# Routing of thirteen tiles moved into the merge stage, and a first gather from expert 0's ranks alone

## Chip, cores and metric

The kernel runs on one core of a Trainium2 chip. The metric is the device time of one execution in microseconds (us).

## The reference, cut to what matters

One encoder layer: two token mixers (banded attention and stick-breaking attention) are merged by gates and projected, then a hierarchical mixture of experts is added. 2048 tokens of width 1024, 4 groups of 8 experts, hidden width 512. Blocks of 128 rows are formed expert by expert.

```python
x = x + (merged @ w_out[layer]).astype(x.dtype)
h2 = rms_norm(x, norm_ffn_g[layer])
...
g_top, g_idx = lax.top_k(g_prob, 1)                  # one group of four
e_top, e_idx = lax.top_k(jax.nn.softmax(e_logits), 2)  # two experts of its eight
e_top = e_top / jnp.sum(e_top, axis=-1, keepdims=True)
weights = (g_top * e_top).reshape(-1)
counts = jax.ops.segment_sum(jnp.ones_like(eid), eid, num_segments=N_EXPERTS)
padded = (counts + ROW_BLOCK - 1) // ROW_BLOCK * ROW_BLOCK
dest = pad_offsets[s_eid] + jnp.arange(n_assign) - offsets[s_eid]
...
return (jax.nn.silu(xr @ w1[e]) * (xr @ w3[e])) @ w2[e]   # per block of 128 rows
```

## The kernel before

The layer runs as four programs one behind the other, each a block with a stream of instructions for each engine: norm and values, projection with banded attention, stick-breaking with gates, the merge stage, and last routing with the experts. This change touches the last two. Every product of the heavy kind is three matmuls (`passes3`), of operands split into a rounded part and a rest (hi, lo) of type fp32r; ScalarE (ACT) rounds, VectorE (DVE) takes the rest.

**Merge stage** (`merge_and_output_projection`). 16 tiles of 128 tokens. For tile n VectorE adds the residual (L1454), ACT and VectorE form the norm, TensorE (PE) turns x (`turn`) and multiplies by the router's weights (`route`), and VectorE takes the 36 logits of each token (L1465). Between these lie the units of the branch products, which end with tile 12 (`units_after`): behind it VectorE and ACT have little to do while TensorE works on `quarter` after `quarter`. In tiles 12 to 14 the first six of eight up-weight pieces of expert 0 are loaded by SP, rounded by ACT (L1412) and split by VectorE (L1511), two to a tile (`early_after`). SP loads piece j only when piece j-2 has been split. `m_lo`, `y_hi` and `y_lo` are tiles of this stage.

**Routing** (`routing_and_experts`, VectorE's list from L1866). On all 16 tiles at once VectorE picks the group and two experts of each token (`first_max` and what is between, 20 chained steps: `Chain` puts a semaphore wait behind each), marks them in OH and their sum O (L1884, L1887, bf16), and TensorE makes from O the counts of each expert (L2018, 16 matmuls with a matrix of ones) and the rank of each token within its expert (L2020, L2022, 16 matmuls), bf16 operands. From these come the number of blocks of each expert, their offsets, and the destination of each row: `lo` is its place in a block, `hi` its block. `row1h` are one-hots of lo (L1926, four instructions of 1024 columns). 32 matmuls of two columns (L2029) sum the tokens of block 0; from them comes the index column of the first gather (L1935), which GpSimd (POOL) issues (L1747). Then for four groups of 8 of the 32 (choice, tile) pairs VectorE makes block one-hots (L1942, 512 columns) and their product with token and weights (L1946, 1536 columns), and TensorE sums them into the table of all blocks (`table(m)`, L2036). VectorE then reads the table (`table()`, L1951 to L1954).

**Experts** (`all_experts`). For each block: TensorE turns the gathered rows (L2046), ACT rounds them (L1806), VectorE splits them (L1959), then up products (L52 to L54 into `ex_ps_h`), silu (L1824), gate (L1979), down products. The weights of the next expert stream in through SP (12 pieces of 512 KB an expert). A piece is loaded when the piece that held its place has been split: L1726 loads expert 1's up pieces and waits for `up_split` for the last two, L1729 loads its down pieces and waits for `down_split`, all in SP's order. ACT rounds expert 1's down pieces (L1819) between its two silus of block 0. What sets the order everywhere is each engine's list as written; no planner changes it.

TensorE's order ahead of the experts: table(0) to table(2), turn of block 0, table(3). VectorE's: four groups of marks, first_up(6), split of x, table(), first_up(7), four down pieces.

## Time and profile before

| what | us |
|---|---|
| median of 3 runs | 2675.66 (2674.98 to 2676.53) |
| the profiled execution | 2677.67 |
| its span | 2675.8 |
| TensorE busy in the span | 2584.5 |
| VectorE busy in the span | 1639.0 |
| ScalarE busy in the span | 1490.5 |

All times of the trace count from the start of the span. Matmul durations overlap, so what counts for a row of them is the distance of their starts. The granted clock is that of TensorE, 1.00 for 2.4 GHz and 0.50 for 1.2 GHz. A "DMA share" of 1 is all 16 DMA engines busy.

### The profile page before, as it was taken

Reading aid. Unit: us, or ns where it says so; the run is one execution under the profiler, and the core shown is the slowest. Engines: PE = TensorE matmul, PEld = TensorE weight load, DVE = VectorE, ACT = ScalarE, POOL = GpSimd, SP = SyncE. Lnnn points to the kernel's source line nnn. Section 1 sums busy time; section 2 is a strip of 40 time slices with the busy share of each in tenths; the row PEclk is TensorE's granted clock in tenths of the full one; section 3 lists DMA queues with packets and bytes.
Section 4 is the critical chain, followed back from the end, with each engine's and each line's share of the span. In section 5 each row is a group of like instructions: output and inputs, shape, how many; then the busy total and the mean of one; then the engine's idle time right before and its main releaser. Section 6 shows DMA issues by size and latency. Waiting matters only on the chain. (4 is left out here: it accounts for less than half of the span.)

```text
span 2675.8 us, 41251 instructions
## 1 busy us (share of the span) xinstructions
PE 2584.5 (97%) x13573; PEld 2157.3 (81%) x13574; DVE 1639.0 (61%) x2218; ACT 1490.5 (56%) x2630; POOL 612.3 (23%) x707
## 2 busy tenths in 40 slices
PE   7999999989999999999899999699999999999997
PEld 6788777778888888888899998577788888888886
...
GB/s 179 132 206 149 126 122 134 145 278 220 196 216 169 188 174 195 194 141 112 228 157 120 134 126 123 170 289 389 323 228 234 243 287 317 324 235 224 228 302 65
DMA packets 197344, 536.67 MB, mean 201 GB/s; under 512 B 20136, under 2 KB 70776, under 8 KB 192736
## 3 DMA queue, kind: packets, MB, share of 16 engines
...
q14 instruction: 50, 0.41, 0.0%
...
## 5 line engine op out<-in xcount | busy, mean ns | idle before, releaser
L1078 POOL TENSOR_TENSOR sb_sig<-sb_sig,sb_R 128x512 f32<-128x512 f32 (+1 forms) x320 | 340.7, 1065 | 409.5 <-DVE sb_R L1018 409.3
L52 PE MATMUL ex_ps_h<-w_region,ex_x_hi 128*128 128x512 f32 x816 | 322.9, 396 | 0.8 <-DVE ex_x_lo L1959 0.8
L54 PE MATMUL ex_ps_h<-w_region,ex_x_lo 128*128 128x512 f32 x816 | 318.8, 391 | 0.0
L53 PE MATMUL ex_ps_h<-w_region,ex_x_hi 128*128 128x512 f32 x816 | 318.6, 390 | 0.0
L1964 DVE TENSOR_TENSOR w_region<-ex_w,w_region 128x1024 fp32r<-128x1024 f32 x248 | 284.9, 1216 | 1.8 <-ACT w_region L1812 1.7
L1018 DVE TENSOR_TENSOR_SCAN sb_R<-sb_z,sb_R,sb_zeros 128x512 f32<-128x512 f32 x192 | 245.7, 1279 | 57.1 <-ACT sb_z L946 56.9
L1969 DVE TENSOR_TENSOR ex_wd_lo<-ex_w,ex_wd_hi 128x1024 fp32r<-128x1024 f32 x200 | 239.6, 1219 | 38.8 <-ACT ex_wd_hi L1819 38.8
L1812 ACT CAST w_region<-ex_w 128x1024 fp32r<-128x1024 f32 x248 | 240.2, 1053 | 9.7 <-DMA ex_w<-in_w_exp 9.4
L958 ACT CAST sb_aT_hi<-sb_pst 128x512 fp32r<-128x512 f32 (+1 forms) x320 | 168.1, 525 | 134.2 <-PE sb_pst L1107 130.9
L1026 DVE TENSOR_TENSOR sb_aT_lo<-sb_pst,sb_aT_hi 128x512 fp32r<-128x512 f32 (+1 forms) x320 | 192.3, 601 | 51.9 <-ACT sb_aT_hi L958 50.0
L945 ACT ACTIVATE sb_sig<-sb_z 128x512 f32<-128x512 f32 (+1 forms) x320 | 172.2, 538 | 85.2 <-PE sb_z L1100 83.8
L1819 ACT CAST ex_wd_hi<-ex_w 128x1024 fp32r<-128x1024 f32 x196 | 196.8, 1060 | 2.2 <-DMA ex_w<-in_w_exp 2.2
L52 PE MATMUL ip_ps<-h_hi,ip_w_hi 128*128 128x512 f32 x448 | 182.4, 407 | 3.5 <-DVE ip_w_lo L605 3.5
L54 PEld LDWEIGHTS ex_ps_h<-w_region,ex_x_lo 128*128 128x128 f32 x816 | 153.6, 188 | 32.3
L52 PEld LDWEIGHTS ex_ps_h<-w_region,ex_x_hi 128*128 128x128 f32 x816 | 153.6, 188 | 31.5 <-issue 1.0
L53 PEld LDWEIGHTS ex_ps_h<-w_region,ex_x_hi 128*128 128x128 f32 x816 | 153.8, 188 | 30.6
L1107 PE MATMUL sb_pst<-sb_ident,sb_sig 128*128 128x128 f32 x1088 | 171.6, 273 | 7.0 <-DVE sb_aT_lo L1026 7.0
L54 PE MATMUL ip_ps<-h_hi,ip_w_lo 128*128 128x512 f32 x448 | 175.8, 392 | 0.0
L53 PE MATMUL ip_ps<-h_lo,ip_w_hi 128*128 128x512 f32 x448 | 175.4, 392 | 0.0
L1107 PEld LDWEIGHTS sb_pst<-sb_ident,sb_sig 128*128 128x128 f32 x1088 | 137.6, 140 | 46.1 <-issue 7.9
L946 ACT ACTIVATE sb_z<-sb_z 128x512 f32<-128x512 f32 (+1 forms) x320 | 171.7, 537 | 0.0
...
## 6 DMA issues: line engine op xcount, KB each, us to landing
...
```

The source lines that it names most:

```text
L52: nc.tensor.matmul(out, w_hi, x_hi, start=first, stop=False)
L53: nc.tensor.matmul(out, w_hi, x_lo, start=False, stop=False)
L54: return nc.tensor.matmul(out, w_lo, x_hi, start=False, stop=last)
L945: nc.scalar.activation(sig[:, j % 5, 0:width], z[:, j % 3, 0:width], ACT.Sigmoid, scale=HD ** -0.5)
L1018: nc.vector.tensor_tensor_scan(R[:, r, first + 1:first + width + 1], z[:, j % 3, 0:width], zeros[:, 0:width], start, ALU.mult, ALU.max).th ...
L1026: nc.vector.tensor_tensor(aT_lo[part], ps_t[:, j % 2, b0 * P:TC].rearrange("p (b s) -> p b s", s=P), aT_hi[part], ALU.subtract).then_inc(l ...
L1078: nc.gpsimd.tensor_tensor(sig[:, j % 5, 0:width], sig[:, j % 5, 0:width], R[:, r, first:first + width], ALU.mult).then_inc(a_done, 1)
L1107: last = nc.tensor.transpose(ps_t[:, j % 2, b * P:(b + 1) * P], sig[:, j % 5, b * P - OFF[j]:(b + 1) * P - OFF[j]], ident[:, :])
L1812: nc.scalar.copy(wu_hi[:, j, :], wr[:, j, :]).then_inc(up_rounded, 1)
L1819: nc.scalar.copy(wd_hi[:, u, k, :], wr[:, KD + k, :]).then_inc(down_rounded, 1)
L1964: nc.vector.tensor_tensor(wu_lo[:, j, :], wr[:, j, :], wu_hi[:, j, :], ALU.subtract).then_inc(up_split, 1)
L1969: nc.vector.tensor_tensor(wd_lo[:, u, k, :], wr[:, KD + k, :], wd_hi[:, u, k, :], ALU.subtract).then_inc(down_split, 1)
```

## The change

The choosing of experts for tiles 0 to 12 (`NTA` = 13) and the one-hots of their ranks move into the merge stage, into the gaps of VectorE behind tile 12; TensorE forms their ranks there (`rank`, ahead of the last tile's product), and forms them a second time at the start of the last program. The tiles OH, O, tri, ones, first and row1h now live in `w_low`, a region that both stages share, and are fp32r instead of bf16. The last program chooses for three tiles only. The first gather takes its rows from the ranks of expert 0 alone: block 0 holds the tokens whose rank in expert 0 is under 128, so no block count is needed, and it has an index tile of its own. Every expert gets at least one block as before. `row1h` of all tiles is one-hot of the rank's low seven bits. In the marking of blocks two instructions for a group become 24 `tensor_scalar` instructions, one for each (tile, component). The order ahead of the experts changes on TensorE (turn first, then all four tables) and on VectorE (two groups of marks, split of x, two groups, table(), down pieces, then both first_ups). The semaphore `y_half_done` goes, its counts move into `br0_done`.

The core of the diff:

```diff
+NTA = NT - 3
...
+            def split_early(j):
+                dve.wait_ge(up_rounded, j + 1)
+                nc.vector.tensor_tensor(w64[:, 1, j, :], up_slots[j % 2], w64[:, 0, j, :],
+                                        ALU.subtract).then_inc(up_split, 1)
+
+            chain = Chain(dve, chosen)
+            NA = 2 * NTA
+            d, lo = (spare[:, NTA * NE + i * NA:NTA * NE + (i + 1) * NA] for i in (0, 2))
+            di = spare[:, NTA * NE + NA:NTA * NE + 2 * NA].bitcast(I32)
+            kept = spare[:, NTA * NE + NA:NTA * NE + 2 * NA].rearrange("p (k t) -> p k t", k=2)
+
+            def rank_rows():
+                V = nc.vector
+                by_expert = spare[:, 0:NTA * NE].rearrange("p (t e) -> p t e", t=NTA)
+                dve.wait_ge(ranked, 1)
+                for k in range(2):
+                    chain(V.tensor_tensor(by_expert, ps_r, OH[:, k, 0:NTA, :, :].rearrange("p t g e -> p t (g e)"), ALU.mult))
+                    chain(V.tensor_reduce(d[:, k * NTA:(k + 1) * NTA], by_expert, AX.X, ALU.add))
+                chain(V.tensor_copy(di, d))
+                chain(V.tensor_single_scalar(di, di, P - 1, ALU.bitwise_and))
+                chain(V.tensor_copy(lo, di))
+                chain(V.scalar_tensor_tensor(kept, d.rearrange("p (k t) -> p k t", k=2), float(P),
+                                             OH[:, :, 0:NTA, 0, 0], ALU.is_lt, ALU.mult))
+                chain(V.tensor_tensor(first, kept.unsqueeze(3).to_broadcast([P, 2, NTA, 2]),
+                                      cst[:, C_TOK:C_TOK + NTA].unsqueeze(1).unsqueeze(3).to_broadcast([P, 2, NTA, 2]),
+                                      ALU.mult))
+
+            def mark_rows():
+                shape = [P, NTA, P]
+                for k in range(2):
+                    chain(nc.vector.tensor_tensor(row1h[:, k, 0:NTA, :],
+                                                  cst[:, C_IOTA:C_IOTA + P].unsqueeze(1).to_broadcast(shape),
+                                                  lo[:, k * NTA:(k + 1) * NTA].unsqueeze(2).to_broadcast(shape),
+                                                  ALU.is_equal))
...
+                if n == NTA:
+                    nc.vector.tensor_copy(tri, cst[:, C_TRI:C_TRI + P])
+                    chain(nc.vector.tensor_copy(ones, cst[:, C_ONES:C_ONES + P]))
+                    mark_experts(nc, chain, OH, O, ohg, oh, 0, NTA).then_inc(O_ready, 1)
+                    split_early(1)
+                if n == NTA + 1:
+                    rank_rows()
+                    split_early(4)
+                if n == NTA + 2:
+                    split_early(5)
...
-                for j in early_after(n):
-                    dve.wait_ge(up_rounded, j + 1)
-                    nc.vector.tensor_tensor(w64[:, 1, j, :], up_slots[j % 2], w64[:, 0, j, :],
-                                            ALU.subtract).then_inc(up_split, 1)
+                if n == NTA - 1:
+                    dve.wait_ge(l_read, NTA)
+                    ohg, oh = choose_experts(nc, chain, logits, cst, 0, NTA, spare, y_flat)
+                    split_early(0)
+                if n == NTA:
+                    split_early(2)
+                    split_early(3)
+                if n == NTA + 1:
+                    mark_rows()
...
+            def rank():
+                pe.wait_ge(weighted, NU)
+                pe.wait_ge(O_ready, 1)
+                nc.tensor.matmul(ps_r, tri, O[:, 0:NTA, :], start=True, stop=False)
+                for t in range(NTA - 1):
+                    last = nc.tensor.matmul(ps_r[:, t + 1:, :], ones,
+                                            O[:, t, :].unsqueeze(1).to_broadcast([P, NTA - 1 - t, NE]),
+                                            start=False, stop=t == NTA - 2)
+                last.then_inc(ranked, 1)
...
+                if n + 2 == NT:
+                    rank()
...
+def routing_views(low):
+    kept = low[:, 0, :, :].rearrange("p k c -> p (k c)")
+    n_oh, n_o = 2 * NT * NE, NT * NE
+    at = n_oh + n_o
+    OH = kept[:, 0:n_oh].rearrange("p (k t g e) -> p k t g e", k=2, t=NT, g=GR)
+    O = kept[:, n_oh:at].rearrange("p (t e) -> p t e", t=NT)
...
+    row1h = low[:, 1, :, :].rearrange("p k c -> p (k c)").rearrange("p (k t r) -> p k t r", k=2, t=NT)
+    return OH, O, tri, ones, first, first_late, late1h, row1h
...
+def choose_experts(nc, ch, logits, cst, t0, t1, real, hot):
+    V, n = nc.vector, t1 - t0
+    bc = lambda ap, width: ap.to_broadcast([P, n, width])
+    cut = lambda ap, at, w: ap[:, at:at + n * w].rearrange("p (t e) -> p t e", t=n)
+    es, key8, key4 = cut(real, 0, EG), cut(real, n * EG, EG), cut(real, n * EG, GR)
...
+    ohg, oh = cut(hot, 0, GR), [cut(hot, n * GR, EG), cut(hot, n * (GR + EG), EG)]
+    G = logits[:, t0:t1, 0:GR]
+    E = logits[:, t0:t1, GR:GR + NE].rearrange("p t (g e) -> p t g e", g=GR)
+    rev4, rev8 = cst[:, C_REV4:C_REV4 + GR], cst[:, C_REV8:C_REV8 + EG]
+
+    def first_max(out1h, src, m, key, rev, width):
+        ch(V.tensor_reduce(m, src, AX.X, ALU.max))
+        ch(V.tensor_tensor(key, src, bc(m.unsqueeze(2), width), ALU.is_equal))
+        ch(V.tensor_tensor(key, key, bc(rev.unsqueeze(1), width), ALU.mult))
+        ch(V.tensor_reduce(gk, key, AX.X, ALU.max))
+        ch(V.tensor_tensor(out1h, key, bc(gk.unsqueeze(2), width), ALU.is_equal))
+
+    first_max(ohg, G, gm, key4, rev4, GR)
+    ch(V.tensor_tensor(G, G, bc(gm.unsqueeze(2), GR), ALU.subtract))
+    ch(V.tensor_tensor(E, E, ohg.unsqueeze(3).to_broadcast([P, n, GR, EG]), ALU.mult))
+    ch(V.tensor_reduce(es, E.rearrange("p t g e -> p t e g"), AX.X, ALU.add))
+    first_max(oh[0], es, mx0, key8, rev8, EG)
+    ch(V.scalar_tensor_tensor(es, oh[0], -3.0e38, es, ALU.mult, ALU.add))
+    first_max(oh[1], es, mx1, key8, rev8, EG)
+    ch(V.tensor_tensor(logits[:, t0:t1, NE], mx1, mx0, ALU.subtract))
+    return ohg, oh
...
+def mark_experts(nc, ch, OH, O, ohg, oh, t0, t1):
+    V, shape = nc.vector, [P, t1 - t0, GR, EG]
+    for k in range(2):
+        ch(V.tensor_tensor(OH[:, k, t0:t1, :, :], ohg.unsqueeze(3).to_broadcast(shape),
+                           oh[k].unsqueeze(2).to_broadcast(shape), ALU.mult))
+    flat = [OH[:, k, t0:t1, :, :].rearrange("p t g e -> p t (g e)") for k in range(2)]
+    return V.tensor_tensor(O[:, t0:t1, :], flat[0], flat[1], ALU.add)
...
-            pool.wait_ge(table_step, FIRST_COLUMN)
-            fetch(0)
+            pool.wait_ge(ix_x_ready, 1)
+            nc.gpsimd.sem_inc(pool_order, 1)
+            nc.gpsimd.indirect_dma_start(xg[:, :], None, h2_d, bass.IndirectOffsetOnAxis(ap=ix_x[:, 0:1], axis=0)) \
+                .then_inc(x_in, 16)
...
+            ohg, oh = choose_experts(nc, ch, logits, cst, NTA, NT, wide, sel)
+            mark_experts(nc, ch, OH, O, ohg, oh, NTA, NT).then_inc(O_ready, 1)
+            dve.wait_ge(O_ready, 1)
+            V.tensor_tensor(first_late, bc(O[:, late, 0:1], [P, NT - NTA, 2]), bc(tok[:, late].unsqueeze(2), [P, NT - NTA, 2]),
+                            ALU.mult)
+            for cols in (slice(0, 1), slice(MAXB + 1, BT)):
+                V.tensor_scalar(idx_all[:, cols], iota[:, cols], 0.0, trash, ALU.mult, ALU.add)
+            V.memset(w_all[:, 0:1], 0.0)
+
+            dve.wait_ge(summed, RANKED)
+            V.tensor_tensor(late1h, bc(iota.unsqueeze(1), [P, NT - NTA, P]), bc(ps_r[:, late, 0:1], [P, NT - NTA, P]),
+                            ALU.is_equal).then_inc(hot_ready, 1)
+            ch(V.tensor_scalar(nblk, ps_c[:, 0:NE], 1.0, float(P - 1), ALU.max, ALU.add))
             ch(V.tensor_copy(di, nblk))
             ch(V.tensor_single_scalar(di, di, 7, ALU.logical_shift_right))
             ch(V.tensor_copy(nblk, di))
             ch(V.tensor_tensor_scan(ends, cst[:, C_ONES:C_ONES + NE], nblk, 0.0, ALU.mult, ALU.add))
             ch(V.tensor_tensor(off, ends, nblk, ALU.subtract))
+
+            dve.wait_ge(summed, FIRST_SUMMED)
+            ch(V.tensor_scalar(tmp[:, 0:1], ps_f[:, 0:1], 0.0, trash1, ALU.is_equal, ALU.mult))
+            V.scalar_tensor_tensor(ix_x[:, :], ps_f[:, 0:1], -1.0, tmp[:, 0:1], ALU.add, ALU.add).then_inc(ix_x_ready, 1)
             V.tensor_copy(blk_tab[:, NE:2 * NE], ends[0:1, :])
+            V.tensor_copy(blk_tab[:, 0:NE], off[0:1, :]).then_inc(table_step, 1)
+            dve.wait_ge(exp_out, 2)
+            ch(V.tensor_reduce(gtop, gs, AX.X, ALU.add))
+            ch(V.tensor_scalar(sd, ed, 1.0, None, ALU.add))
+            ch(V.scalar_tensor_tensor(dest, bc(off.unsqueeze(1), [P, NT, NE]), float(P), ps_r, ALU.mult, ALU.add))
             for k in range(2):
+                ch(V.tensor_tensor(by_expert, dest, OH[:, k, :, :, :].rearrange("p t g e -> p t (g e)"), ALU.mult))
                 ch(V.tensor_reduce(d[:, k * NT:(k + 1) * NT], by_expert, AX.X, ALU.add))
             ch(V.tensor_copy(di, d))
             V.tensor_single_scalar(hi_i, di, 7, ALU.logical_shift_right)
             ch(V.tensor_single_scalar(lo_i, di, P - 1, ALU.bitwise_and))
             V.tensor_copy(hi, hi_i)
             ch(V.tensor_copy(lo, lo_i))
+            shape = [P, 2, NT - NTA, P]
+            V.tensor_tensor(row1h[:, :, late, :], bc(iota.unsqueeze(1).unsqueeze(1), shape),
+                            bc(lo.rearrange("p (k t) -> p k t", k=2)[:, :, late].unsqueeze(3), shape),
+                            ALU.is_equal).then_inc(hot_ready, 1)
+            V.reciprocal(gtop, gtop)
+            ch(V.reciprocal(sd, sd))
+            ch(V.tensor_tensor(w[:, 0, :], gtop, sd, ALU.mult))
+            for k in range(2):
+                V.tensor_copy(vals[:, k, :, 0], tok)
+            ch(V.tensor_tensor(w[:, 1, :], w[:, 0, :], ed, ALU.mult))
             ch(V.tensor_copy(vals[:, :, :, 1], w[:, :, :]))
             ch(V.tensor_tensor(vals[:, :, :, 2], w[:, :, :], vals[:, :, :, 1], ALU.subtract))
+
+            def mark_blocks(m):
+                k, part = GROUPS[m]
                 if m >= 2:
                     dve.wait_ge(hot_used, m - 1)
+                for i in range(GA):
+                    t = part * GA + i
+                    for c3 in range(3):
+                        last = V.tensor_scalar(rows1h[:, m % 2, i, c3, :], iota[:, 0:64], hi[:, k * NT + t:k * NT + t + 1],
+                                               vals[:, k, t, c3:c3 + 1].bitcast(F32), ALU.is_equal, ALU.mult)
+                last.then_inc(hot_ready, 1)
 
             def table():
+                dve.wait_ge(h2_stored, NT * 16 + 32)
                 dve.wait_ge(hot_used, NA // GA)
...
-            first_up(NEARLY)
+            mark_blocks(0)
+            mark_blocks(1)
             split_x(0)
+            mark_blocks(2)
+            mark_blocks(3)
             table()
-            for j in range(NEARLY + 1, KD):
-                first_up(j)
             for k in range(KF):
                 down_piece(0, 0, k)
+            for j in range(NEARLY, KD):
+                first_up(j)
             dve.wait_ge(table_step, BOUNDS)
...
+            late, NL = slice(NTA, NT), NT - NTA
+            nc.tensor.matmul(ps_r[:, 0:NTA, :], tri, O[:, 0:NTA, :], start=True, stop=False)
+            for t in range(NTA - 1):
+                nc.tensor.matmul(ps_r[:, t + 1:NTA, :], ones, O[:, t, :].unsqueeze(1).to_broadcast([P, NTA - 1 - t, NE]),
+                                 start=False, stop=t == NTA - 2)
+            for t in range(NTA):
+                nc.tensor.matmul(ps_r[:, late, :], ones, O[:, t, :].unsqueeze(1).to_broadcast([P, NL, NE]),
+                                 start=t == 0, stop=False)
+            for t in range(NTA):
+                nc.tensor.matmul(ps_c[:, 0:NE], ones, O[:, t, :], start=t == 0, stop=False)
+            for k in range(2):
+                for t in range(NTA):
+                    nc.tensor.matmul(ps_f, row1h[:, k, t, :], first[:, k, t, :], start=k == t == 0, stop=False)
             pe.wait_ge(O_ready, 1)
+            nc.tensor.matmul(ps_r[:, late, :], tri, O[:, late, :], start=False, stop=False)
+            for t in range(NTA, NT - 1):
+                nc.tensor.matmul(ps_r[:, t + 1:, :], ones, O[:, t, :].unsqueeze(1).to_broadcast([P, NT - 1 - t, NE]),
+                                 start=False, stop=t == NT - 2)
+            for t in range(NTA, NT):
+                last = nc.tensor.matmul(ps_c[:, 0:NE], ones, O[:, t, :], start=False, stop=t == NT - 1)
             last.then_inc(summed, 1)
+            pe.wait_ge(hot_ready, 1)
+            for i in range(NL):
+                last = nc.tensor.matmul(ps_f, late1h[:, i, :], first_late[:, i, :], start=False, stop=i == NL - 1)
             last.then_inc(summed, 1)
 
             def table(m):
+                k, part = GROUPS[m]
+                pe.wait_ge(hot_ready, m + 3)
                 for i in range(GA):
+                    last = nc.tensor.matmul(ps_b[:, 0:192], row1h[:, k, part * GA + i, :],
                                             rows1h[:, m % 2, i, :, :].rearrange("p c b -> p (c b)"),
+                                            start=m == i == 0, stop=m == len(GROUPS) - 1 and i == GA - 1)
                 last.then_inc(hot_used, 1)
 
...
-            for m in range(NA // GA - 1):
+            turn_x(0)
+            for m in range(len(GROUPS)):
                 table(m)
-            turn_x(0)
-            table(NA // GA - 1)
             pe.wait_ge(table_step, BOUNDS)
             all_experts(pe, lambda e, first: None, rows)
```

## Rows read from the trace of the kernel before

**Rows 1.** Table of stretches: us, busy us of each engine (instructions), granted clock, DMA share.

```profile
1716.00:1721.00 5.00, 4.21 (x32) 2.54 (x32) 3.63 (x20) 5.00 (x6) 0.00 (x0) 0.54 1.03 401
1721.00:1726.00 5.00, 0.00 (x0) 0.00 (x0) 4.72 (x12) 0.50 (x1) 0.00 (x0) 0.80 0.77 304
1726.00:1734.00 8.00, 6.99 (x32) 6.90 (x32) 4.78 (x12) 0.00 (x0) 0.00 (x0) 0.50 0.00 1
1734.00:1747.00 13.00, 9.40 (x40) 8.70 (x40) 11.55 (x11) 1.01 (x1) 2.24 (x2) 0.50 0.19 54
1747.00:1751.00 4.00, 3.30 (x8) 2.63 (x9) 3.93 (x8) 0.00 (x0) 1.72 (x2) 0.50 0.42 110
1807.00:1927.00 120.00, 115.50 (x535) 92.60 (x534) 96.09 (x101) 87.57 (x108) 26.84 (x31) 1.00 0.98 368
1927.00:2647.00 720.00, 720.00 (x3419) 599.37 (x3418) 503.75 (x548) 463.51 (x587) 151.73 (x205) 1.00 0.75 252
```

**Rows 2.** VectorE in order of time, new block: start, us, line, operands; idle before in brackets.

```profile
1703.09 0.26 DVE L1465 SCALAR_TENSOR_TENSOR logits<-mo_ps_l,mo_small,rt_bias 128x36 f32<-128x36 f32 x1 [1.45 <-PE mo_ps_l L1575]
1707.18 0.22 DVE L1866 TENSOR_REDUCE w_stage<-logits 128x16 f32<-128x64 f32 x1 [3.84 <-PEq L1188]
...
1713.99 0.17 DVE L1881 TENSOR_TENSOR w_stage<-w_stage 128x16 f32<-128x16 f32 x1
...
1733.89 0.16 DVE L1935 SCALAR_TENSOR_TENSOR idx_all<-ex_ps_g,rt_cst 128x1 int32<-128x1 f32 x1
1733.97 0.68 DVE L1942 TENSOR_TENSOR w_stage<-rt_cst,ex_g 128x512 f32<-128x512 f32 x1
...
1743.91 1.22 DVE L1974 TENSOR_TENSOR w_region<-ex_w,w_region 128x1024 fp32r<-128x1024 f32 x1
1746.34 1.22 DVE L1959 TENSOR_TENSOR ex_x_lo<-ex_ps_x,ex_x_hi 128x1024 fp32r<-128x1024 f32 x1 [1.21 <-ACT ex_x_hi L1806]
```

**Rows 3.** TensorE: one line of its source view, then its timeline ahead of the experts.

```profile
L2029 PE MATMUL ex_ps_g<-rt_first,ex_wd_hi x32: 352/352/374, 1726.5 to 1733.2; 128*128 128x2 f32 x32
...
1741.53 2.02 PE L2036 MATMUL ex_ps_g<-ex_wd_lo,ex_wd_hi 128*128 128x192 f32 x8 [0.49 <-DVE ex_wd_lo L1946]
1743.35 1.91 PE L2046 MATMUL ex_ps_x<-ex_ident,w_stage 128*128 128x128 f32 x8
...
1747.70 0.79 PE L52 MATMUL ex_ps_h<-w_region,ex_x_hi 128*128 128x512 f32 x1 [0.79 <-DVE ex_x_lo L1959]
```

**Rows 4.** VectorE timeline: instructions with per-partition operand, then two without, neither pair chained.

```profile
399.00 0.88 DVE L565 SCALAR_TENSOR_TENSOR ba_qn<-ba_q,ba_gq,ba_rq 128x256 f32<-128x256 f32 x2 [4.70 <-ACT ba_rk L475]
399.80 0.41 DVE L567 SCALAR_TENSOR_TENSOR ba_kn<-ba_k,ba_gk,ba_rk 128x192 f32<-128x192 f32 x1
...
1724.52 0.18 DVE L1917 TENSOR_SCALAR ex_g<-ex_g 128x32 int32<-128x32 int32 x1
1724.61 0.17 DVE L1918 TENSOR_SCALAR ex_g<-ex_g 128x32 int32<-128x32 int32 x1
```

**Rows 5.** Last tiles of the merge stage: VectorE, then TensorE.

```profile
1657.54 0.43 DVE L1448 TENSOR_TENSOR mo_m_lo<-mo_gates,mo_m_hi 128x256 fp32r<-128x256 f32 x1
...
1666.82 1.23 DVE L1454 TENSOR_TENSOR mo_rows<-mo_ps,mo_rows 128x1024 f32<-128x1024 f32 x1 [2.81 <-PE mo_ps L54]
...
1683.37 0.50 PE L52 MATMUL mo_ps<-mo_wo_hi,mo_m_hi 128*128 128x512 f32 x1 [1.32 <-DVE mo_rows L1454]
```

**Rows 6.** Restart: VectorE, SP and ACT timelines, then a line of the DMA view.

```profile
1749.45 4.62 DVE L1969 TENSOR_TENSOR ex_wd_lo<-ex_w,ex_wd_hi 128x1024 fp32r<-128x1024 f32 x4
...
1707.53 2.77 SPq L1711 DMA_DIRECT2D ex_w<-in_w_exp  x6
...
1750.70 3.73 SPq L1729 DMA_DIRECT2D ex_w<-in_w_exp  x4
...
1762.07 1.05 ACT L1819 CAST ex_wd_hi<-ex_w 128x1024 fp32r<-128x1024 f32 x1 [1.22 <-DMA ex_w<-in_w_exp]
...
w_stage<-h,ex_ix_x POOLq DMA_INDIRECT x1, 5.2
```

161 lines of the change are left out of this document (42 added, 119 removed).

## The prediction

> **What bounds the kernel now.** I read the profile from the outside in. First the table of stretches: after 1927 us TensorE is busy in every one of 720 us, and from 1807 to 1927 it is busy for 115.5 of 120 us with the DMA engines at 0.98 [rows 1]. So what a change ahead of the experts saves or costs goes to the end of the kernel nearly whole, as an earlier or later start. The place of the change is the hole between the two: the last logits at 1703.09, the first instruction of the next block at 1707.18 [rows 2], the first expert matmul at 1747.70 [rows 3]. In this hole VectorE is the bound most of the time, as its list shows: twenty chained steps of choosing from 1707.18 to 1714.2, then ranks and one-hots, the index of the first gather at 1733.89, four groups of block marking from 1733.97 to 1743.91, the split of x at 1746.34 [rows 2]. TensorE waits for it, and runs at the lower clock, 1.2 GHz: granted 0.50 from 1726 to 1747 [rows 1].
>
> **What moves into the merge stage, and what it costs there.** Choosing for thirteen tiles is the same twenty steps on 13/16 of the columns: the fixed part stays, so 6.5 us for 7.0 [rows 2]. It starts when the last m is split (1657.97) and ends at about 1664.4; the split of the first expert piece behind it ends at 1665.7, and the next norm wants VectorE at 1666.82 [rows 5]. It is hidden by 1.2 us. The marking of experts (2.3 us), rank_rows (3.6) and mark_rows (two instructions of 1664 columns, 3.9 us) fall into the two like gaps of the next tiles; the pieces are loaded some microseconds later through SP's queue, since each load waits for a split, but they are wanted only by splits that the order has put later too. I take 0. If one of these covers were gone, the cost would be its overhang, 1 to 2 us. TensorE's rank() is thirteen matmuls with fp32 weights at the higher clock, 1.65 us, in a hole of 1.32 us ahead of the last tile [rows 5], which began at about 1682.05: **+0.3 us**.
>
> **The new block: TensorE first.** Choosing for three tiles takes VectorE 20 short steps of about 0.2 us and the marking 0.8 us, so O is ready at about 1712.4. But the index of the first gather waits for the ranks of all tiles (the semaphore summed), and they stand in TensorE's queue behind a prefix: 13 matmuls for the early ranks again, 13 for the late tiles' offset, 13 for the counts, 26 for the first rows. These are 65, and the operands are now fp32r, no longer bf16. The nearest rows: 32 matmuls with fp32r weights and 2 columns began from 1726.5 to 1733.2, one in (1733.2-1726.5)/31 = 0.216 us, at clock 0.50 [rows 1, 3]; with 192 columns eight took 2.02 us, hardly more. I price 61 at 0.216 and the four widest (416, 384, 352, 320 columns at 1.2 GHz) by their columns, 0.35 to 0.27, together 14.4 us: 1707.2 to 1721.6. Six more for the last tiles, 1.3 us, and a tail of 0.15: **ranks at 1723.1**, about 2 us later than before, where the 32 matmuls for them lie between 1716 and 1721 [rows 1], and VectorE idle for 10 us ahead of it. Behind this wait in VectorE's queue stands all the rest.
>
> **VectorE after that wait.** late1h (384 columns, 0.5 us), six chained steps to the block offsets (1.35), two for the index (0.45): the index is ready at 1725.4, 8.7 us earlier than the 1734.05 of before [rows 2]. Before the marking come five instructions of 512 columns at 0.72 with their gap (3.6 us; 0.69 is the 512-column row [rows 2]), one of 768 columns (0.9) and some fourteen short ones (2.8): 7.3 us, to 1732.7. What is the early gather worth? Its landing takes 5.2 us from issue [rows 6]; with 1.1 us on GpSimd it is in at 1731.7, turned at 1733.6 [rows 3], rounded at 1734.6. VectorE comes to split_x(0) only after two groups of marks, at about 1741. So the early gather is hidden anyway and I credit **nothing** for it.
>
> **The marks decide.** Before, a group is two instructions, and four groups took 1743.91-1733.97 = 9.94 us [rows 2]. After, a group is 24 tensor_scalar instructions of 64 columns, each with two per-partition operands, 96 in all. No row shows this form. Bounds: without such operands two tensor_scalars of 32 columns began 0.09 apart, at 1724.52 and 1724.61; with one, the instructions of 256 columns began 0.40 apart, which is 0.267 for the columns and 0.133 fixed [rows 4]. So one operand costs some 0.05. The low bound is 0.11 (none counts), with one counting 0.133+0.033 = 0.166, with two counting 0.22, and 0.25 if the 64 columns go at one in a cycle. I take 0.18, just above the row of one operand: 96 x 0.18 = **17.3 us, 7.3 more than before**.
> The Trainium skill, "Vector Engine (DVE) Microarchitecture Reference", section 5.2, gives about 75 ns fixed for an instruction and 1.04 ns a column; as an estimate 96 x 0.142 = 13.6 us, and my sum would end 3.7 us lower. The page "VectorE: DVE Perf Modes", in its rules for kernel authors, speaks against this part of the change: it says to keep the number of instructions small. The 0.09 us floor in the rows agrees with that.
>
> **The sum to the first expert matmul.** 1732.7 + 17.3 + 1.1 (split_x) = 1751.1; the last table(3) on TensorE, which now stands behind the last marks instead of beside the split, 2.0 [rows 3]; first expert matmul at 1753.2, against 1747.7: +5.5.
>
> **The restart of the weight stream.** Call T the start of VectorE's table(). Before T is 1747.5, and first_up(6) has run before it. After it, table (0.8), four down pieces at 1.13 (the row of four, 4.62 us), then both first_ups. SP's queue is in order: it waits for those two splits before it issues expert 1's last two up pieces and only then the four down pieces. So the two go at T+6.6 and T+7.7, the down pieces from T+8.2 about 0.45 apart (six issues in 2.77 us), the last at T+9.5. Before, the last was issued near 1754.1, T+6.6, and ACT could round it at 1762.07, 8.0 us later [rows 6]. The same 8.0 gives T+17.5 for T+14.6: ACT's rounding of it stands ahead of the second silu, so block 0 and the next loads of SP start 2.9 us later. With the DMA engines at 0.98 afterwards I don't let this be absorbed: **+3** (0 if the burst lands faster than the spread loads did, 5 if it collides with the first scatter).
>
> **Total**: 0.3 + 5.5 + 3.0 = +8.8 us. The profiled execution took 2677.67 with a span of 2675.8, 2.0 over the median of 2675.66. Difference on the median: **2684.5 us**.
>
> **Rivals.** (1) The clock. It rose once in this hole: during or right after the 32 rank and count matmuls between 1716 and 1721: 0.54 over these 5 us, 0.80 over the next 5. In the 32 with 2 columns, and in the 40 from 1734 to 1747, it stayed at 0.50 [rows 1, 3]. The prefix begins like the first and goes on like the second. If it rose 4.2 us in and stayed, the rest of the prefix halves: ranks at 1717.3, -5.8, **2678.6**, no change. The Trainium skill, "TensorE: Matmul & The Clock Gate", Part 1, says that sustained work releases the throttle; by it this rival is the likely one. The two runs at 0.50 speak against. (2) Cheap marks: 0.11 instead of 0.18, -6.7, **2677.7**, no change. The two 32-column instructions at 0.09 speak for it, the one-operand rows against. (3) Dear marks, 0.22 to 0.25: +3.8 to +6.7, about **2690**. (4) The other side, faster: TensorE at the higher clock from the prefix through to the experts. Then ranks come at 1714.6 (-8.5), table(3) takes half (-1.0), and the first matmuls of block 0, run at 0.50 until 1751, lose nothing (-1.7): -11.2, and it turns faster by 0.2% from marks at 0.15 down; with 0.133 it is -15.7, **2668.7**. Speaks against: before, the first matmuls of this block found the clock down, 0.54 over their stretch [rows 1]. (5) The chain moves and nothing comes of it: the DMA-bound stretch takes up a delay of the start, as its 4.5 us of idle TensorE suggest, **2676 to 2680**.
>
> **How the numbers follow.** A measurement of this kernel can tell about 0.2%, 5.4 us, from no change. My forecast (2681 to 2688.5) 0.44; (1) 0.13; (2) 0.12; (3) 0.14; (4) 0.10; (5) 0.07. Faster takes (4) and some luck elsewhere, 0.14; slower takes the forecast, (3) and no more, 0.58; same the rest, 0.28. The range for 8 in 10 leaves out the far ends of (3) and (4): 2671 to 2691.
>
> **What would show it.** Right: the first matmuls after the block start about 0.216 apart at granted clock 0.50, and the last of the counts near 1723; VectorE idle about 10 us ahead of late1h; the gather's index near 1725.4 but the first expert matmul later than 1747.7; 96 TENSOR_SCALAR records that take 16 to 21 us; expert 1's down pieces landing 17 us after table(). Wrong: PEclk at 1.00 between 1711 and 1723, marks under 13 us, a norm of tiles 13 to 15 that starts later than before (1666.82 and two more), or TensorE idle less in the first block than before.

## The result

The changed kernel takes 2692.18 us (median of 4, 2691.39 to 2693.13) against 2675.32 us before (4 runs, 2674.22 to 2676.53): ratio 1.0065, 95% interval 1.0052 to 1.0077. It is slower, by about twice what was forecast (+8.8 us), and its time lies 1.2 us beyond the range. The profiled execution has a span of 2691.3 us, 15.5 more than before.

VectorE of the changed kernel in order of time, from the start of the last program to table():

```profile
1706.30 0.17 DVE L1717 TENSOR_REDUCE ex_s<-logits 128x3 f32<-128x12 f32 x1 [2.39 <-PEq L1191]
...
1722.33 0.56 DVE L1991 TENSOR_TENSOR w_low<-rt_cst,ex_ps_h 128x384 fp32r<-128x384 f32 x1 [10.30 <-PE ex_ps_h L2130]
...
1724.41 0.16 DVE L2002 SCALAR_TENSOR_TENSOR ex_ix_x<-ex_ps_g,rt_cst 128x1 int32<-128x1 f32 x1
...
1731.86 10.79 DVE L2037 TENSOR_SCALAR ex_wd_hi<-rt_cst,ex_g,rt_vals 128x64 fp32r<-128x64 f32 x48
...
1743.70 10.79 DVE L2037 TENSOR_SCALAR ex_wd_hi<-rt_cst,ex_g,rt_vals 128x64 fp32r<-128x64 f32 x48
1756.68 0.28 DVE L2044 TENSOR_SCALAR rt_cst<-ex_ps_g,rt_cst 128x64 f32<-128x64 f32 x1 [2.18 <-PE ex_ps_g L2141]
```

They answer to [rows 2]. The choosing starts at 1706.30 and is done early, but VectorE then stands idle for 10.30 us until TensorE has the ranks (1722.33). The index of the first gather is there at 1724.57, 9.5 us earlier than before. The marks, 9.94 us before, are two rows of 48 instructions, 10.79 us each. Then TensorE, from its first matmul of the program, and the first expert matmul:

```profile
1706.60 0.69 PE L2112 MATMUL ex_ps_h<-w_low 128*128 128x416 f32 x1 [2.98 <-PEq L1191]
1707.08 2.84 PE L2114 MATMUL ex_ps_h<-w_low 128*128 128x384 f32 x12
1709.76 2.99 PE L2117 MATMUL ex_ps_h<-w_low 128*128 128x96 f32 x13
1712.55 2.92 PE L2120 MATMUL ex_ps_h<-w_low 128*128 128x32 f32 x13
1715.31 5.69 PE L2123 MATMUL ex_ps_g<-w_low 128*128 128x2 f32 x26
...
1756.73 0.79 PE L52 MATMUL ex_ps_h<-w_region,ex_x_hi 128*128 128x512 f32 x1 [0.17 <-issue]
```

These are the 65 prefix matmuls: the first 13 with 416 down to 32 columns, then 13, 13 and 26 that begin 0.21 us apart whether they have 96, 32 or 2 columns. The first expert matmul is at 1756.73 instead of 1747.70 [rows 3]. The restart of the weight stream, as VectorE, SP, GpSimd, ACT and TensorE show it (SP's row is expert 1's four down pieces, GpSimd's the first scatter, ACT's two round the second and the last of those down pieces, TensorE's is the first down product of block 0):

```profile
1762.08 2.35 DVE L2067 TENSOR_TENSOR w_region<-ex_w,w_region 128x1024 fp32r<-128x1024 f32 x2
...
1783.52 1.23 DVE L2052 TENSOR_TENSOR ex_x_lo<-ex_ps_x,ex_x_hi 128x1024 fp32r<-128x1024 f32 x1 [1.93 <-ACT ex_x_hi L1923]
...
1764.82 2.13 SPq L1846 DMA_DIRECT2D ex_w<-in_w_exp  x4
...
1765.55 1.62 POOL L1875 DMA_INDIRECT out_x<-w_stage,ex_ix_y  x1 [3.36 <-ACT w_stage L1964]
...
1774.61 1.04 ACT L1936 CAST ex_wd_hi<-ex_w 128x1024 fp32r<-128x1024 f32 x1 [2.10 <-DMA ex_w<-in_w_exp]
...
1777.88 1.05 ACT L1936 CAST ex_wd_hi<-ex_w 128x1024 fp32r<-128x1024 f32 x1 [0.21 <-DMA ex_w<-in_w_exp]
...
1777.38 0.79 PE L52 MATMUL ex_ps_y<-ex_wd_hi,ex_g_hi 128*128 128x512 f32 x1 [8.43 <-DVE ex_g_lo L2077]
```

VectorE's two late up splits end at 1764.43; SP, which waits for them, issues the last two up pieces and then the four down pieces at 1764.82, 0.7 us ahead of the scatter. Before, the last down piece was rounded at 1762.07 [rows 6], now at 1777.88. TensorE is idle for 8.43 us ahead of its first down product. That product needs the gated values g, and in ACT's list the rounding of their first half stands behind the second down piece of expert 1, which was rounded at 1774.61. The table of stretches (us, busy us of PE, PEld, DVE, ACT and POOL with instructions, granted clock, DMA share, GB/s):

```profile
1706.00:1722.00 16.00, 15.40 (x71) 15.42 (x71) 4.95 (x27) 10.14 (x11) 0.00 (x0) 0.50 0.91 347
1764.00:1778.00 14.00, 5.57 (x25) 4.26 (x24) 3.84 (x6) 4.20 (x6) 1.62 (x1) 0.79 0.83 262
1776.00:1780.00 4.00, 2.62 (x6) 2.01 (x7) 3.24 (x5) 2.37 (x3) 0.00 (x0) 0.50 0.20 76
1807.00:1927.00 120.00, 116.60 (x544) 94.35 (x542) 106.63 (x112) 96.80 (x117) 28.92 (x32) 1.00 1.03 387
```

The clock stays at 0.50 in the prefix, and behind the hole TensorE starts at 0.50 again. Because executions differ by some microseconds in when the last program starts, the runs are compared by distances from its first VectorE instruction. The last distance, to the end of the span, is of one execution each:

| run | ranks there (late1h) | first expert matmul | split of block 1's x | end of the span | time against the kernel before |
|---|---|---|---|---|---|
| before | | 40.5 | 59.1 | 968.6 | 1 |
| changed | 16.0 | 50.4 | 77.2 | 985.0 | 1.0065 (1.0052 to 1.0077) |
| a_marks2 | 16.0 | 38.9 | 66.2 | 973.9 | 1.0028 (1.0018 to 1.0038) |
| a_order | 16.0 | 50.5 | 70.8 | 979.3 | 1.0034 (1.0021 to 1.0046) |
| a_sporder | 16.1 | 50.5 | 67.1 | 978.2 | 1.0035 (1.0022 to 1.0047) |
| a_both | 16.0 | 38.9 | 56.5 | 966.4 | 0.9995 (0.9985 to 1.0005) |
| a_rankfirst | 10.5 | 44.9 | 71.4 | 979.2 | 1.0050 (1.0033 to 1.0066) |
| a_bf16 | 8.0 | 42.4 | 67.6 | 977.3 | 1.0043 (1.0029 to 1.0057) |
| a_lategather | 16.0 | 50.5 | 77.3 | 984.6 | 1.0066 (1.0049 to 1.0083) |
| b_marks24 | | 50.0 | 67.8 | 977.1 | 1.0041 (1.0027 to 1.0055) |
| best | 5.7 | 27.7 | 47.6 | 956.0 | 0.9962 (0.9949 to 0.9976) |

One thousandth is 2.7 us. All runs named a_ start from the changed kernel, b_ from the one before.

### The profile page after: what moved, and what is told of

The parts are those of the page before. It is cut to its first block and busy times, and to the rows that moved or that the text cites. A ratio compares the mean times of both kernels' runs of the same rounds, so it can differ in the third digit from the quotient of the medians.

```text
span 2691.3 us, 41412 instructions
## 1 busy us (share of the span) xinstructions
PE 2592.8 (96%) x13596; PEld 2167.7 (81%) x13597; DVE 1656.9 (62%) x2338; ACT 1490.9 (55%) x2628; POOL 611.4 (23%) x706
## 5 line engine op out<-in xcount | busy, mean ns | idle before, releaser
L2062 DVE TENSOR_TENSOR w_low<-ex_w,ex_wd_hi 128x1024 fp32r<-128x1024 f32 x200 | 239.6, 1219 | 46.1 <-ACT ex_wd_hi L1936 46.1
L52 PE MATMUL ex_ps_y<-ex_wd_hi,ex_g_hi 128*128 128x512 f32 x408 | 164.6, 403 | 9.2 <-DVE ex_g_lo L2077 9.2
```

The lines of the kernel that those rows point to most:

```text
L52: nc.tensor.matmul(out, w_hi, x_hi, start=first, stop=False)
L2062: nc.vector.tensor_tensor(wd_lo[:, u, k, :], wr[:, KD + k, :], wd_hi[:, u, k, :], ALU.subtract).then_inc(down_split, 1)
```

## Experiments: the marks

**a_marks2**, the changed kernel with two instructions for a group.

```diff
...
+                ch(V.tensor_tensor(blk1h, bc(iota[:, 0:64].unsqueeze(1), [P, GA, 64]),
+                                   bc(hi[:, own].unsqueeze(2), [P, GA, 64]), ALU.is_equal))
                 if m >= 2:
                     dve.wait_ge(hot_used, m - 1)
-                for i in range(GA):
-                    t = part * GA + i
-                    for c3 in range(3):
-                        last = V.tensor_scalar(rows1h[:, m % 2, i, c3, :], iota[:, 0:64], hi[:, k * NT + t:k * NT + t + 1],
-                                               vals[:, k, t, c3:c3 + 1].bitcast(F32), ALU.is_equal, ALU.mult)
-                last.then_inc(hot_ready, 1)
+                V.tensor_tensor(rows1h[:, m % 2, :, :, :], bc(blk1h.unsqueeze(2), [P, GA, 3, 64]),
+                                bc(val[:, own, :].unsqueeze(3), [P, GA, 3, 64]), ALU.mult).then_inc(hot_ready, 1)
```

> The changed kernel with the block marks made as before: two instructions a group (512 and 1536 columns) in place of 24 tensor_scalars. Theory M (the 24 instructions at 0.225 us each are the largest term): four groups take 10 us instead of 21.6, the first expert matmul comes 11.6 us earlier, at about 1745, and since the stream of weights restarts from VectorE's table() the end moves with it: about 2680.5 against 2692 of the changed kernel. Rival R (TensorE's tables and the order of the restart set the time whatever VectorE does): under 3 us gained.

```profile
1732.08 0.69 DVE L2038 TENSOR_TENSOR ex_wd_hi<-rt_cst,ex_g 128x512 fp32r<-128x512 f32 x1
1732.80 1.76 DVE L2042 TENSOR_TENSOR ex_wd_hi<-ex_wd_hi,rt_vals 128x1536 fp32r<-128x1536 f32 x1
...
1745.36 0.79 PE L52 MATMUL ex_ps_h<-w_region,ex_x_hi 128*128 128x512 f32 x1 [0.16 <-issue]
```

A group is 0.69 and 1.76 us again, and the first expert matmul comes 38.9 us after the start instead of 50.4: 11.5 us earlier, as expected. Of this the end shows 0.0037 of the time, 9.9 us (the difference of two ratios, each good to 3 us); in the two traces the last program is 11.1 us shorter. Rival R, under 3 us, falls.

**b_marks24**, the other way round: the kernel before with the 24 instructions alone.

```diff
-                ch(V.tensor_tensor(blk1h, bc(iota[:, 0:64].unsqueeze(1), [P, GA, 64]),
-                                   bc(hi[:, part].unsqueeze(2), [P, GA, 64]), ALU.is_equal))
...
+                for i in range(GA):
+                    a = m * GA + i
+                    for c3 in range(3):
+                        last = V.tensor_scalar(rows1h[:, v, i, c3, :], iota[:, 0:64], hi[:, a:a + 1],
+                                               val[:, a, c3:c3 + 1].bitcast(F32), ALU.is_equal, ALU.mult)
+                last.then_inc(hot_ready, 1)
```

> The kernel before with one part of the change alone: 24 tensor_scalars a group for the marks. Theory M: 21.6 us for four groups instead of 9.94, all of it on the path: 11.6 us slower, about 1.0043 of before. If part of the marks' cost in the changed kernel came from its other order: 8 us or less.

```profile
1730.04 21.48 DVE L1945 TENSOR_SCALAR ex_wd_lo<-rt_cst,ex_g,rt_vals 128x64 fp32r<-128x64 f32 x96
...
1753.92 0.79 PE L52 MATMUL ex_ps_h<-w_region,ex_x_hi 128*128 128x512 f32 x1 [1.21 <-DVE ex_x_lo L1959]
```

96 instructions in 21.48 us, 11.5 more than before, and the first expert matmul at 50.0 us instead of 40.5, so 9.5 of them are on the path: the marks begin 0.7 us sooner after the start, and the split of x, which had waited 1.21 us for ACT [rows 2], finds its operand ready. The whole is 11.0 us slower by the ratio (7 to 15 by its interval), 8.5 by the distance to the end of the span. The traces put it between the two expectations, and the ratio can't tell these apart. The marks alone so cost about as much as my whole forecast of +8.8.

**a_pointers** prices the instruction by its operands.

```diff
+                        a = hi[:, k * NT + t:k * NT + t + 1] if m in (0, 1) else -1.0
+                        b = vals[:, k, t, c3:c3 + 1].bitcast(F32) if m in (0, 2) else 0.0
+                        last = V.tensor_scalar(rows1h[:, m % 2, i, c3, :], iota[:, 0:64], a, b, ALU.is_equal, ALU.mult)
```

> Prices the disputed instruction by its operands. The changed kernel, with the 24 tensor_scalars of the four groups in four forms: group 0 with two per-partition operands as in the change, group 1 with the first one only (the factor is an immediate 0), group 2 with the second one only (the compared value is an immediate -1), group 3 with none. Groups 1 to 3 so mark nothing: the rows of three quarters of the (choice, tile) pairs are left out of the table. If each per-partition operand costs 0.058 us: 0.225, 0.166, 0.166 and 0.11 us an instruction, the four groups 5.4, 4.0, 4.0 and 2.6 us. If the first operand carries the whole price, groups 0 to 2 are alike. If the price lies in the 64 columns at one a cycle and not in the operands, all four are alike at 0.2 or more.

Its VectorE list, four rows of 24 with the split of x between:

```profile
1730.95 5.44 DVE L2039 TENSOR_SCALAR ex_wd_hi<-rt_cst,ex_g,rt_vals 128x64 fp32r<-128x64 f32 x24
1736.31 3.99 DVE L2039 TENSOR_SCALAR ex_wd_hi<-rt_cst,ex_g 128x64 fp32r<-128x64 f32 x24
...
1741.35 3.98 DVE L2039 TENSOR_SCALAR ex_wd_hi<-rt_cst,rt_vals 128x64 fp32r<-128x64 f32 x24
1745.24 2.53 DVE L2039 TENSOR_SCALAR ex_wd_hi<-rt_cst 128x64 fp32r<-128x64 f32 x24
```

Groups 1 to 3 of this kernel mark nothing, so three quarters of the rows are missing from its table, and only the length of these rows is read from it. From start to start a group of two operands takes 5.36 us, 0.223 an instruction; with either one alone 3.90 and 3.89, 0.163; with none (2.53-0.2)/23 = 0.10. So each per-partition operand costs 0.06 us, and the second as much as the first. This is the upper of the two bounds that I had (0.22), at the higher rate for the columns. The Trainium skill, "VectorE: DVE Perf Modes", tier table, gives tensor_scalar on fp32 in SBUF twice the rate of tensor_tensor. The trace agrees: without such operands 64 columns begin 0.10 us apart and the 32 columns of [rows 4] 0.09, so 32 columns more cost 0.01 to 0.02 us, where the tensor_tensor rows of 512 and 1536 columns (0.69 and 1.76 us) give 0.033. The Trainium skill, "Vector Engine (DVE) Microarchitecture Reference", section 5.2, gives about 75 ns fixed and 1.04 ns a column. As an estimate from both pages, 64 columns at twice that rate make 0.108 us, and the trace agrees for the form without such operands (0.10). By this estimate 96 marks would have been 10.4 us and not 21.6.

## Experiments: the restart of the weight stream

**a_order** puts VectorE's list behind the marks back.

```diff
             mark_blocks(3)
+            first_up(NEARLY)
             table()
+            for j in range(NEARLY + 1, KD):
+                first_up(j)
             for k in range(KF):
                 down_piece(0, 0, k)
-            for j in range(NEARLY, KD):
-                first_up(j)
```

> The changed kernel with VectorE's order behind the marks as before: first_up(6) ahead of table(), then table(), first_up(7), then the four down pieces. Nothing else moves. Theory B (the burst of six loads late in SP's queue costs what the trace shows: expert 1's last down piece rounded 21.2 us after table() instead of 14.6): 6 to 7 us gained, about 2685.5. Rival (my blind term of 3 us was right and the rest is the marks): 3 us, 2689. Second rival (DMA-bound stretch takes it up): 0 to 1 us.

SP's issues of expert 1's last two up pieces and four down pieces, and ACT's rounding of the last:

```profile
1756.01 3.45 SPq L1843 DMA_DIRECT2D ex_w<-in_w_exp  x2
1760.26 4.21 SPq L1846 DMA_DIRECT2D ex_w<-in_w_exp  x4
...
1772.21 1.05 ACT L1936 CAST ex_wd_hi<-ex_w 128x1024 fp32r<-128x1024 f32 x1 [0.39 <-DMA ex_w<-in_w_exp]
```

The pieces go out spread over 8.5 us, the last is rounded 15.2 us after table() instead of 21.2, and block 1's x is split 6.4 us earlier. The time is 8.3 us less by the ratios, and the distance to the end of the span 5.7 us less. So the part of the restart that this order makes is some 6 us, twice the 3 that I had for all of it.

**a_sporder** keeps VectorE's list and changes SP's only.

```diff
-            for j in range(KD):
-                if j >= NEARLY:
-                    sp.wait_ge(up_split, j + 1)
+            for j in range(NEARLY):
                 sp.dma_start(wr[:, j, :], w_pieces[NPC + j, :, :]).then_inc(w_in[j], 16)
             for k in range(KF):
...
+            for j in range(NEARLY, KD):
+                sp.wait_ge(up_split, j + 1)
+                sp.dma_start(wr[:, j, :], w_pieces[NPC + j, :, :]).then_inc(w_in[j], 16)
```

> The changed kernel, VectorE's order kept, but SP issues expert 1's four down pieces ahead of its last two up pieces. It tells whether the order of VectorE's splits or the blocking in SP's queue makes the burst. Theory B: the down pieces go out as each split ends, 1.1 us apart from about 2 us after table(), block 0 loses its hole of 7 us on TensorE: 5 to 7 us gained. Rival (the splits themselves are what block 0 waits for, through VectorE): under 2 us.

```profile
1758.16 3.73 SPq L1844 DMA_DIRECT2D ex_w<-in_w_exp  x4
1762.70 1.46 SPq L1847 DMA_DIRECT2D ex_w<-in_w_exp  x2
...
1767.37 2.17 ACT L1937 CAST ex_wd_hi<-ex_w 128x1024 fp32r<-128x1024 f32 x2 [0.25 <-DMA ex_w<-in_w_exp]
```

The four down pieces leave from 1758.16 on as each is split, the last is rounded by 1769.54, and block 1's x is split 10.1 us earlier than in the changed kernel. It is therefore the wait in SP's queue, ahead of four issues that had nothing to do with it, and not VectorE's own time. The time gains 8.0 us by the ratios, no more than a_order did, and the distance to the end of the span 6.8 of the 10.1 us: from 1807 to 1927, TensorE idles 5.0 us here and 3.4 us in the changed kernel. So some of what the start gains seems to be lost in the DMA-bound stretch; one execution each shows it.

**a_both** puts marks and VectorE's order back together (the two edits above).

> Marks as before and VectorE's order as before, the rest of the change kept. If the two terms add up: 11.6 + 6.5 = 18 us gained, about 2674, within 2 us of the kernel before: the early gather and the routing in the merge stage then bring nothing by themselves, since TensorE's fp32r prefix holds the ranks until 1722. If a third cost is hidden in the change: 2678 or more. If the part that was moved brings something: 2670 or less.

Ratio 0.9995 (0.9985 to 1.0005): no difference from the kernel before can be measured. The two terms add (9.9 + 8.3 = 18.2 of 18.7 us), and what else is in the change neither costs nor earns a net amount that can be measured. The first expert matmul comes 1.6 us earlier than before: that is what the moved routing, its prefix on TensorE, the early gather and TensorE's new order earn together.

## Experiments: why the moved routing earns so little

**a_rankfirst** puts the 26 two-column matmuls behind the ranks, and the index of the gather behind VectorE's chain.

```diff
-            for k in range(2):
-                for t in range(NTA):
-                    nc.tensor.matmul(ps_f, row1h[:, k, t, :], first[:, k, t, :], start=k == t == 0, stop=False)
             pe.wait_ge(O_ready, 1)
...
             last.then_inc(summed, 1)
+            for k in range(2):
+                for t in range(NTA):
+                    nc.tensor.matmul(ps_f, row1h[:, k, t, :], first[:, k, t, :], start=k == t == 0, stop=False)
             pe.wait_ge(hot_ready, 1)
```

> The changed kernel with TensorE's 26 two-column matmuls for block 0 moved behind the ranks and counts in its queue, and the gather's index computed by VectorE behind its routing chain, just ahead of the marks. Theory P (VectorE's 10.3 us of idle time are the fp32r prefix on TensorE, 0.216 us a matmul at the lower clock): the ranks come 5.6 us earlier, late1h at about 1716.7 instead of 1722.3, marks and first expert matmul 5.5 us earlier, about 2686.5 against 2692. Rival (VectorE waits for the late tiles' O or something else by then): late1h moves under 1 us.

```profile
1710.67 0.17 DVE L1717 TENSOR_REDUCE ex_s<-logits 128x3 f32<-128x12 f32 x1 [2.83 <-PEq L1191]
...
1721.15 0.55 DVE L1991 TENSOR_TENSOR w_low<-rt_cst,ex_ps_h 128x384 fp32r<-128x384 f32 x1 [4.75 <-PE ex_ps_h L2127]
```

This program started late, so only distances count: ranks 10.5 us after the start instead of 16.0, first expert matmul 44.9 instead of 50.4. Both moved by the 5.5 us expected, and the distance to the end of the span by 5.8. The time gained 4.0 us by the ratios, which within the intervals can't be told from 5.5.

**a_bf16** gives the rank and count matmuls bf16 operands.

```diff
+        O = sb("rt_O", [P, NT, NE], BF16)
+        tri_b, ones_b = sb("rt_tri", [P, P], BF16), sb("rt_ones", [P, P], BF16)
...
+            nc.scalar.copy(tri, cst[:, C_TRI:C_TRI + P])
+            nc.scalar.copy(ones, cst[:, C_ONES:C_ONES + P])
+            nc.scalar.copy(O[:, 0:NTA, :], O_early[:, 0:NTA, :].bitcast(F32)).then_inc(exp_out, 1)
...
+            pe.wait_ge(exp_out, 1)
```

> The changed kernel with bf16 copies of O, tri and ones for the rank and count matmuls of the last program (ACT makes them at its start, about 1 us; the 26 for block 0 stay fp32r and in place). Theory P: 39 of the 65 prefix matmuls go by their columns instead of 0.216 us, ranks 5 to 6 us earlier, about 2686.5. If the time of a small matmul does not depend on the type of its weights: plus 1 us from the copies, 2693.

TensorE's list, one stretch of the table, and VectorE's first instruction and late1h:

```profile
1710.57 2.29 PE L2121 MATMUL ex_ps_h<-rt_O,rt_ones 128*128 128x384 bf16 x12
1712.69 1.00 PE L2124 MATMUL ex_ps_h<-rt_O,rt_ones 128*128 128x96 bf16 x13
1713.53 0.48 PE L2127 MATMUL ex_ps_h<-rt_O,rt_ones 128*128 128x32 bf16 x13
1713.86 3.06 PE L2130 MATMUL ex_ps_g<-w_low 128*128 128x2 f32 x26
...
1714.00:1717.00 3.00, 3.00 (x32) 3.00 (x32) 0.94 (x6) 2.99 (x3) 0.00 (x0) 0.96 0.99 385
...
1709.28 0.17 DVE L1717 TENSOR_REDUCE ex_s<-logits 128x3 f32<-128x12 f32 x1 [2.19 <-PEq L1191]
...
1717.24 0.56 DVE L1997 TENSOR_TENSOR w_low<-rt_cst,ex_ps_h 128x384 fp32r<-128x384 f32 x1 [2.23 <-PE ex_ps_h L2137]
```

13 matmuls with 32 columns take 0.48 us in place of 2.92. And more than expected: the 26 with two columns, still fp32r, take 3.06 us in place of 5.69, since the granted clock was 0.96 (the 2.4 GHz level) over their stretch: it had risen by 1714, behind 38 bf16 matmuls in 3.3 us. The ranks and the first expert matmul come 8.0 us earlier, not 5.5, and the time is 5.9 us less by the ratios. With the fp32r prefix it had stayed at 0.50 for 16 us. So the clock rival was right in its mechanism and wrong for this kernel: the prefix as it was written did not bring the clock up, the bf16 one did. The Trainium skill, "TensorE: Matmul & The Clock Gate", Part 1, has sustained matmul activity release the throttle; by that rule alone the fp32r prefix would have been at 1.2 GHz only in its first part, and the table of the changed kernel speaks against it (0.50 from 1706 to 1722, with PE busy for 15.40 of 16 us). What it is in the two prefixes that makes the difference was not tried apart.

**a_lategather** undoes the early gather alone (VectorE computes the index behind its chain).

```diff
-            dve.wait_ge(summed, FIRST_SUMMED)
-            ch(V.tensor_scalar(tmp[:, 0:1], ps_f[:, 0:1], 0.0, trash1, ALU.is_equal, ALU.mult))
-            V.scalar_tensor_tensor(ix_x[:, :], ps_f[:, 0:1], -1.0, tmp[:, 0:1], ALU.add, ALU.add).then_inc(ix_x_ready, 1)
...
             ch(V.tensor_tensor(vals[:, :, :, 2], w[:, :, :], vals[:, :, :, 1], ALU.subtract))
+            dve.wait_ge(summed, FIRST_SUMMED)
+            ch(V.tensor_scalar(tmp[:, 0:1], ps_f[:, 0:1], 0.0, trash1, ALU.is_equal, ALU.mult))
+            V.scalar_tensor_tensor(ix_x[:, :], ps_f[:, 0:1], -1.0, tmp[:, 0:1], ALU.add, ALU.add).then_inc(ix_x_ready, 1)
```

> The changed kernel with the index of the first gather computed 7 us later, behind VectorE's routing chain and ahead of the marks. Theory (the early gather is hidden behind two groups of marks): within 1 us of the changed kernel, the index at about 1731.5 instead of 1724.5 and the first expert matmul where it was. If the early gather is worth what the change is named for: 5 to 7 us slower.

```profile
1731.82 0.16 DVE L2028 SCALAR_TENSOR_TENSOR ex_ix_x<-ex_ps_g,rt_cst 128x1 int32<-128x1 f32 x1
...
1737.36 1.94 PE L2151 MATMUL ex_ps_x<-ex_ident,w_stage 128*128 128x128 f32 x8 [13.60 <-DMA w_stage<-h,ex_ix_x]
```

The index is 7.4 us later, block 0 is turned 7.5 us later, and the first expert matmul is at 50.5 us after the start as before the edit; ratio 1.0066 against 1.0065. The early gather, the second thing that the change is named for, is worth nothing here.

**best** joins what was found: the edits of a_marks2, a_order, a_rankfirst and a_bf16, all marks and first_up(6) ahead of the split of x, and TensorE's turn of block 0 between table(1) and table(2).

```diff
-            mark_blocks(0)
-            mark_blocks(1)
-            split_x(0)
-            mark_blocks(2)
-            mark_blocks(3)
+            for m in range(len(GROUPS)):
+                mark_blocks(m)
+            first_up(NEARLY)
+            split_x(0)
...
-            turn_x(0)
             for m in range(len(GROUPS)):
+                if m == 2:
+                    turn_x(0)
                 table(m)
```

> All terms found put right at once: choosing and ranks in the merge stage as in the change; bf16 operands for ranks and counts; the 26 matmuls for block 0 behind them; index of the first gather behind VectorE's chain; marks by two instructions a group, all four ahead of the split of x; first_up(6) ahead of it too; order of the restart as before. If the terms add: ranks at 6 to 8 us after the block's start instead of 16, first expert matmul some 28 us after it (before: 40.5), and about 12 us less than the kernel before: 2663, ratio 0.9955. If the gather, now late, becomes what block 0 waits for: 3 us less gained. If the DMA-bound stretch behind takes it up: ratio 0.998 or more.

```profile
1705.34 0.17 DVE L1717 TENSOR_REDUCE ex_s<-logits 128x3 f32<-128x12 f32 x1 [2.57 <-PEq L1191]
...
1711.06 0.56 DVE L1997 TENSOR_TENSOR w_low<-rt_cst,ex_ps_h 128x384 fp32r<-128x384 f32 x1
...
1733.04 0.49 PE L52 MATMUL ex_ps_h<-w_region,ex_x_hi 128*128 128x512 f32 x1 [1.21 <-DVE ex_x_lo L2062]
```

The ranks are no longer waited for (5.7 us after the start, VectorE comes to them without idle time), the first expert matmul is at 27.7 us, 12.8 us earlier than in the kernel before, and the time is 2664.05 us against 2675.64: ratio 0.9962 (0.9949 to 0.9976), 10.2 us less by the ratio and 11.6 by the medians. From the start of the last program to the end of the span it is 956.0 us against 968.6, 12.6 less: so what the start gained reached the end of the profiled execution, and nothing was lost in the DMA-bound stretch. The 10.2 differ from this by less than the interval (6.4 to 13.6 us). The split of x begins without idle time, so the late gather isn't waited for either. How much each of the joined edits gives here was not tried apart.

## The prediction, step by step

**In the merge stage: right.** VectorE's rows of tile 12, 14 and 15 and TensorE's rank():

```profile
1663.41 1.22 DVE L1480 TENSOR_TENSOR w_region<-mo_y,w_region 128x1024 fp32r<-128x1024 f32 x1
1665.78 1.22 DVE L1464 TENSOR_TENSOR mo_rows<-mo_ps,mo_rows 128x1024 f32<-128x1024 f32 x1 [1.14 <-PE mo_ps L54]
...
1691.05 3.81 DVE L1508 TENSOR_TENSOR w_low<-rt_cst,mo_gates 128x1664 fp32r<-128x1664 f32 x2
...
1681.00 1.61 PE L1643 MATMUL mo_ps_m<-w_low 128*128 128x384 f32 x12
...
1696.49 1.22 DVE L1464 TENSOR_TENSOR mo_rows<-mo_ps,mo_rows 128x1024 f32<-128x1024 f32 x1 [1.64 <-PE mo_ps L54]
...
1703.65 0.26 DVE L1475 SCALAR_TENSOR_TENSOR logits<-mo_ps_l,mo_small,rt_bias 128x36 f32<-128x36 f32 x1 [1.77 <-PE mo_ps_l L1635]
```

The choosing ended at 1663.4 and the split at 1664.6, 1.15 us ahead of the norm (1.2 forecast). mark_rows took 3.81 us (3.9), rank() 1.8 us from 1680.82 (1.65). No norm waited: VectorE is idle ahead of each. From the norm of tile 14 to that of tile 15 it was 15.47 us instead of 15.30, so rank() cost 0.2 us (forecast 0.3).

**TensorE's prefix: right.** Ranks 16.0 us after the start; forecast 1723.1-1707.2 = 15.9. The row of 32 two-column matmuls [rows 3] was the right price for the forms of 96, 32 and 2 columns (0.21 us measured), and the first 13, which have up to 416 columns, took 3.16 us (forecast 3.17).

**VectorE's chain and the early gather: right.** From late1h to the first mark 9.5 us (forecast 9.6), and nothing from the gather, which a_lategather showed. Its rows were there sooner than forecast: TensorE turned them from 1729.85, 23.6 us after the start, where the prediction has them in at 1731.7, 24.5 after it. Nothing hung on that.

**The marks: the step that failed first.** "I take 0.18, just above the row of one operand": it was 0.225, 21.6 us for 96 where the sum had 17.3. The mechanism stood and the term was mis-sized by 4.3 us. The bounds were right; what I took between them rested on the row of one operand, though the form has two, and the step per operand (0.05) had been worked out two sentences earlier.

**The restart: the step that failed worst.** "The same 8.0 gives T+17.5": the last down piece was issued at about T+10 (forecast T+9.5), but rounded at T+21.2. Its transfer took 11 us and not 8. Six pieces and the first scatter came at once: in the 14 us from 1764 the DMA engines moved 262 GB/s at a share of 0.83, in the later stretch 387. I had used the landing time of the last of four loads that were issued 1.1 us apart for one at the end of a burst. By the queues of the DMA view, the six pieces took 64.2% of the engines' time in those 14 us, which is 9.0 us, and the scatter 18.8%, 2.6 us. So most of the engines' time went to the pieces themselves; how fast they land without the scatter was not tried.

The path was wrong too. I had ACT's rounding of the last down piece hold block 0, but TensorE's hole ended with g, which waited for the second piece. From the first expert matmul to the rounding of that piece it was 17.9 us instead of 10.9 (before, it was rounded at 1758.56), +7.0; from there to the split of block 1's x 8.9 instead of 7.8, +1.2, with TensorE at 0.50 behind the hole (2.62 us of work shown in 1776 to 1780 at that clock), for which the sum had no term. The last piece was nearly as late for it: the second half of g was ready at 1779.66, 0.4 us before TensorE came to it. In all, from the first expert matmul to the split of block 1's x it was 26.8 us instead of 18.6, +8.2 where I had +3 and a bound of 5.

**Absorption: partly.** At the split of block 1's x the changed kernel was 17.2 us behind, at the end of the span 15.5. From 1807 to 1927 TensorE idled 3.4 us instead of 4.5 [rows 1]. What rival (5) names was real but small, 1.7 us.

In all: +8.8 forecast; +4.3 from the marks and +5.2 from the restart give 18.3, less 1.7 absorbed; an earlier start of the last program in this execution (0.9 us) takes it to 15.7, beside the 15.5 of the spans. Of the rivals, (3) alone came true, at 0.225 near its lower end. Alone it would have given 2688.8, inside the range. The restart went past its own bound of 5, and the two together lay beyond the range, which let no two unknowns go wrong at once.
